# Bounds loaded one behind each gate-and-up loop, gate and up weights in one transfer, first norm beside the gated projections

## The reference

```python
shift, scale, gate = adaln(c[:, None, :], w_ada, b_ada)
h = rms_norm(x, norm_g) * (1 + scale) + shift
hc = rms_norm(xc, norm_g) * (1 + cscale) + cshift
u = h @ w_in
a_val, a_gate = u[..., :A_WIDTH], u[..., A_WIDTH:AB_Q_OFF]
```

```python
hid = jax.nn.silu(xblk @ w_gate[e]) * (xblk @ w_up[e])
return hid @ w_down[e]
```

## Time and profile before

| | |
|---|---|
| median of 3 runs | 4255.51 us (4252.32 to 4255.72) |
| profiled execution | 4245.79 us, its span 4243.7 us |
| mean granted clock of TensorE | 0.965 |
| TensorE busy | 3750.0 us (88%) |
| VectorE, ScalarE, GpSimd busy | 41%, 23%, 6% |
| HBM read and written | 594.70 MB and 46.92 MB |
| gate and up loads by ScalarE | 120, 2048 KB each, 16.6 us from issue to landing |
| down loads by ScalarE | 60, 2048 KB each, 17.2 us |
| write of zeros to y_tok | 12800 KB, 36.3 us |

### The profile page before, as it was taken

The page is one execution under the profiler, slowest core; times in us unless marked ns, Lnnn a source line. Parts: engine busy times, 40 slices in busy tenths (PEclk is TensorE's granted clock), DMA queues, the critical chain, the costliest instruction groups (busy, mean ns, idle before and its releaser), DMA issues.

```text
span 4243.7 us, 81332 instructions
## 1 busy us (share of the span) xinstructions
PE 3750.0 (88%) x29964; PEld 2095.4 (49%) x29965; DVE 1724.6 (41%) x3835; ACT 975.1 (23%) x2286; POOL 272.6 (6%) x453
## 2 busy tenths in 40 slices
PE   5997888999999889999988969989499998899874
PEld 3564665555444555444565445555344444455443
DVE  2585666413202664152465334434331114343335
ACT  3003545302001332131053212222120002222211
POOL 0000000000000000000000021111100000211111
PEclk9998999999999999999999989999799998999997
DMA  8111222101101000110142178999511113799994
GB/s 314 44 40 40 100 88 113 70 24 40 59 20 40 1 1 11 50 48 31 60 160 102 75 283 354 425 426 425 221 40 40 40 61 120 318 366 418 426 426 150
DMA packets 94333, 644.11 MB, mean 152 GB/s; under 512 B 18640, under 2 KB 41240, under 8 KB 60752
## 3 DMA queue, kind: packets, MB, share of 16 engines
q10 hardware_dynamic: 28896, 386.28, 21.5%
q1 hardware_dynamic: 46928, 194.98, 12.4%
q0 software_dynamic: 18336, 60.44, 4.1%
HBM read 594.70 MB, written 46.92 MB: 151 GB/s over the span
## 4 chain that ended last, share of the span: by engine, by line
PE 37%; DMA 13%; DVE 4%; issue 3%; SPq 2%; ACT 1%; DVEq 1%; ACTq 1%; POOLq 0%; POOL 0%
PE banks L258 23%; DMA y_tok<-arena 7%; PE banks L2407 7%; DMA arena<-in_w_gu 4%; SPq L2360 2%; PE banks L2416 2%; DMA arena<-y_tok,arena 1%; PE banks L1519 1%; DVE arena L1634 1%; PE banks L2122 1%; PE banks L2402 1%; PE banks L467 1%; DMA h_tok<-arena 0%; PE banks L2398 0%; ACTq L2300 0%
## 5 line engine op out<-in xcount | busy, mean ns | idle before, releaser
L258 PE MATMUL banks<-arena 128*128 128x512 f32 (+2 forms) x4544 | 1750.0, 547 | 39.0 <-ACTq L137 16.9
L258 PEld LDWEIGHTS banks<-arena 128*128 128x128 f32 x4544 | 841.4, 191 | 935.6 <-issue 884.6
L2407 PE MATMUL banks<-arena 128*32 128x256 f32 x10240 | 611.1, 387 | 48.2 <-DMA arena<-in_w_gu 41.1
L2407 PEld LDWEIGHTS banks<-arena 128*32 128x32 f32 x10240 | 324.4, 111 | 278.9 <-issue 104.8
L2416 PE MATMUL banks<-arena 128*32 128x256 f32 x5120 | 302.5, 384 | 65.4 <-DVE arena L2561 40.9
L2416 PEld LDWEIGHTS banks<-arena 128*32 128x32 f32 x5120 | 167.8, 110 | 194.0 <-DVE arena L2561 94.3
L1588 PE MATMUL banks<-arena 128*64 128x128 f32 x1952 | 161.8, 285 | 54.9 <-ACT arena L1601 39.2
L945 DVE SCALAR_TENSOR_TENSOR arena<-arena 128x1024 f32<-128x1024 f32 x240 | 195.9, 879 | 0.2 <-DVEq L137 0.2
L301 DVE SCALAR_TENSOR_TENSOR arena<-banks,arena 128x512 f32<-128x512 f32 (+1 forms) x72 | 51.9, 721 | 333.3 <-PE banks L258 333.3
L2373 POOL DMA_INDIRECT arena<-h_tok,arena x176 | 172.1, 978 | 142.2 <-POOL arena L2370 141.4
L1519 PE MATMUL banks<-arena 64*128 64x256 f32 (+2 forms) x768 | 130.1, 470 | 37.7 <-ACT arena L1690 32.8
(11 more groups left out here) (327 smaller groups left out, 3500.8 us busy)
## 6 DMA issues: line engine op xcount, KB each, us to landing
arena<-in_w_gu ACTq DMA_DIRECT2D x120, 2048.0 KB, 16.6
arena<-in_w_dn ACTq DMA_DIRECT2D x60, 2048.0 KB, 17.2
arena<-in_w_ada SPq DMA_DIRECT2D x24, 2048.0 KB, 7.3
y_tok<-arena SPq DMA_DIRECT2D x648, 32.0 KB
arena<-in_w_gu SPq DMA_DIRECT2D x8, 2048.0 KB, 10.8
y_tok<-arena POOLq DMA_DIRECT2D x1, 12800.0 KB, 36.3
arena<-in_ab_w_ada SPq DMA_DIRECT2D x6, 2048.0 KB, 9.5
arena<-in_cd_w_ada SPq DMA_DIRECT2D x6, 2048.0 KB, 7.3
```

The source lines that it names most:

```text
L258: last = pe.matmul(self.bank_of(g, n), lhsT, rhs, start=k == 0, stop=k == KT - 1)
L2407: last = pe.matmul(bank(2 + j)[32 * q:32 * q + 32, 0:256], xbT[:, 128 * j + 32 * q2:128 * j + 32 * q2 + 32], w_gu[slot][j][:, 4 * q2 + q], ...
```

## The change

Three edits. **The stage `ab_norm` goes.** TensorE takes the projection with `N_AB` as its norm, so it waits for each tile of h (`nrm_h`) when it first needs it. GpSimd's small memsets come before the close of `ab_mod`, so the scratch of `M_AB` moves by 10240 words, and the zeros wait for VectorE's last division.

**Gate and up are one transfer** of 128 rows of 32768 B, with one semaphore for each slot. **The bounds are read one at a time:** of the two that each engine read behind the gate-and-up loop of the odd expert, the second is now read behind that of the even one.

```diff
-        M_AB = Mods(("ab",), STAGE)
+        M_AB = Mods(("ab",), STAGE + 10240)
...
                     for k in range(KT):
                         a.wait_ge(nrm_x, KT * i + k + 1)
                         a.activation(h_of[w_][:, k, t0:t0 + n], h_of[w_][:, k, t0:t0 + n], ACT.Identity,
-                                     scale=self.scale(k, w_), bias=self.shift(k, w_))
+                                     scale=self.scale(k, w_), bias=self.shift(k, w_)).then_inc(nrm_h, 1)
+
+            def made(self, rows, k):
+                i = 2 if rows[1] is h_c else rows[2] // 512
+                return KT * i + k + 1
...
-            def load_gu(self, eng, slot, e, part):
-                eng.dma_start(mem(SLOTS[slot] + UNIT * part, UNIT),
-                              t["w_gu"][self.l, bass.ds(e, 1), :, UNIT * part:UNIT * part + UNIT].rearrange(
-                                  "e p n -> p (e n)")).then_inc((self.wa, self.wb)[part][slot], 16)
+            def load_gu(self, eng, slot, e):
+                eng.dma_start(mem(SLOTS[slot], 2 * UNIT), t["w_gu"][self.l, bass.ds(e, 1)].rearrange("e p n -> p (e n)")
+                              ).then_inc(self.wg[slot], 16)
...
                     c0, c1, c2 = bring()
-                    c3, c4 = first(2 * p + 1, 1, c1, c2, p, lambda: [self.cum(eng, 2 * p + 3), self.cum(eng, 2 * p + 4)])
+                    c3 = first(2 * p + 1, 1, c1, c2, p, lambda: self.cum(eng, 2 * p + 3))
                     second(2 * p, 0, c0, c1, p)
-                    first(2 * p + 2, 0, c2, c3, p + 1)
+                    c4 = first(2 * p + 2, 0, c2, c3, p + 1, lambda: self.cum(eng, 2 * p + 4))
                     second(2 * p + 1, 1, c1, c2, p)
                     carry((c2, c3, c4))
...
                     nth = i // 2 if nth is None else nth
-                    pe.wait_ge(self.wa[slot], 16 * nth + 16)
-                    pe.sem_inc(passed, 1)
-                    pe.wait_ge(self.wb[slot], 16 * nth + 16)
+                    pe.wait_ge(self.wg[slot], 16 * nth + 16)
                     pe.sem_inc(passed, 1)
...
                     if following:
-                        for part in range(2):
-                            self.load_gu(a, slot, e, part)
+                        self.load_gu(a, slot, e)
...
             mod_pe(pe, N_AB)
             close("ab_mod")
-            close("ab_norm")
-            P_AB_A.pe(pe)
+            P_AB_A.pe(pe, N_AB)
             close("ab_gated")
...
             N_AB.act(a)
-            close("ab_norm")
             P_AB_A.act(a)
...
             N_AB.divide(d, 2)
-            close("ab_norm")
             conv = conv_dve(d)
...
-            close("ab_mod")
             for ct in range(4):
                 for a0, n in ((0, HALF), (HALF + S, 2 * HALF), (S + L + 3 * HALF, HALF)):
                     g.memset(G_U[:, ct, a0:a0 + n], 0.0)
-            close("ab_norm")
-
+            close("ab_mod")
+            g.wait_ge(nrm_x, nrm_total[0])
             g.memset(zeros, 0.0).then_inc(pool_done, 1)
```

More of the change, by code:

```diff
@@ L536, in mod_dve @@
             M_AB.finish(d, link)
-        nrm_sq, nrm_mm, nrm_rt, nrm_x, nrm_rc = (sem(s_) for s_ in ("nrm_sq", "nrm_mm", "nrm_rt", "nrm_x", "nrm_rc"))
+        nrm_sq, nrm_mm, nrm_rt, nrm_x, nrm_rc, nrm_h = (
+            sem(s_) for s_ in ("nrm_sq", "nrm_mm", "nrm_rt", "nrm_x", "nrm_rc", "nrm_h"))
         nrm_total = [0, 0]
@@ L583, in act @@
                         a.activation(h_of[w_][:, k, t0:t0 + n], h_of[w_][:, k, t0:t0 + n], ACT.Identity,
-                                     scale=self.scale(k, w_), bias=self.shift(k, w_))
+                                     scale=self.scale(k, w_), bias=self.shift(k, w_)).then_inc(nrm_h, 1)
+            def made(self, rows, k):
+                i = 2 if rows[1] is h_c else rows[2] // 512
+                return KT * i + k + 1
         N_AB = Norm(True, lambda k, w_: gs["ab"][:, k, w_:w_ + 1], lambda k, w_: mod["ab"][:, k, w_:w_ + 1])
-        nrm_h, nrm_add, nrm_rd = sem("nrm_h"), sem("nrm_add"), sem("nrm_rd")
-        flow = dict(sq=nrm_total[0], mm=nrm_total[1], rt=nrm_total[1], rc=nrm_total[1], x=nrm_total[0], h=0, add=0,
+        nrm_add, nrm_rd = sem("nrm_add"), sem("nrm_rd")
+        flow = dict(sq=nrm_total[0], mm=nrm_total[1], rt=nrm_total[1], rc=nrm_total[1], x=nrm_total[0], h=nrm_total[0], add=0,
                     rd=0)
@@ L2081, in __init__ @@
                 s = block_sem
-                self.wa, self.wb, self.wd = ([s(f"{w_}_slot{j}") for j in range(2)]
-                                             for w_ in ("w_half_a", "w_half_b", "w_down"))
+                self.wg, self.wd = ([s(f"{w_}_slot{j}") for j in range(2)] for w_ in ("w_gate_up", "w_down"))
                 self.ix, self.xg = s("ix"), [sem(f"moe{l}_x_gathered{i}") for i in range(4)]
@@ L2331, in in_turn @@
                 c0, c1, c2 = bring()
-                c3, c4 = first(E - 3, 1, c1, c2, None, lambda: [self.cum(eng, E - 1), self.cum(eng, E)])
+                c3 = first(E - 3, 1, c1, c2, None, lambda: self.cum(eng, E - 1))
                 second(E - 4, 0, c0, c1)
-                first(E - 2, 0, c2, c3)
+                c4 = first(E - 2, 0, c2, c3, None, lambda: self.cum(eng, E))
                 second(E - 3, 1, c1, c2)
@@ L2341, in blocks_sp @@
                 sp.wait_ge(stage_end, closed(("ev_attn", "od_conv")[self.l]))
-                for part in range(2):
-                    self.load_gu(sp, 1, 0, part)
+                self.load_gu(sp, 1, 0)
                 sp.wait_ge(stage_end, closed(("ev_out", "od_out")[self.l]))
-                for part in range(2):
-                    self.load_gu(sp, 0, E - 1, part)
+                self.load_gu(sp, 0, E - 1)
                 self.load_dn(sp, 0, E - 1)
@@ L2952, in _ @@
             close("m1_sum_final")
-STAGES = ["loads", "ab_mod", "ab_norm", "ab_gated", "ab_qkv", "ab_heads", "ab_attn", "ab_z",
+STAGES = ["loads", "ab_mod", "ab_gated", "ab_qkv", "ab_heads", "ab_attn", "ab_z",
           "ab_out_cd_f", "cd_four", "cd_qkv", "cd_attn", "cd_z", "cd_out_ev_in", "ev_attn",
```

## The result

| kernel | median us | of runs | ratio to before, 95% interval |
|---|---|---|---|
| before | 4255.51 | 4252.32 to 4255.72 | |
| changed | 4309.22 | 4305.97 to 4309.56 | 1.0126 [1.0103, 1.0149] |

The account below looks back on a forecast made before the run. In the expert stages full DMA engines, shared packet by packet by weights and stores, nearly balance TensorE; stores end the first. 4245.8 - 12.9 - 5.5 + 41 + 42 = 4310 us, given as 4320 for the median of runs, range 4231 to 4365 us.

Parts of the forecast that it names:

- The sign and the cause: Expert stages: slower, chance 0.65, because a 32 KB weight row is one packet and one turn, leaving stores fewer turns.
- The room: First expert stage: VectorE's room for eight blocks is gone after some four of eleven pairs, then VectorE and TensorE stop.
- The sum: Whole kernel against the profiled execution: 4245.8 - 12.9 - 5.5 + 41 + 42 = 4310 us.
- the norm: Start of the kernel: TensorE's first projection begins at 63.3 us in place of 76.16 us, 12.9 us sooner.
- The stages: Both expert stages: the long row costs 41 us in the first and 42 us in the second; bounds give back 5.5 us.
- The long row: Expert weights: 32 KB rows as one packet each cost +41 us in the first stage, +42 us in the second.
- The turns: Stores beside full weight queues: 608 turns become 405 in the first stage, a block every 10 us instead of 7.0.
- The bounds: Expert loops where TensorE sets the pace: reading bounds one at a time gains 1.1 us a pair, 5.5 us in all.
- ScalarE's single issue: TensorE's second block after the even expert's gate-and-up loop: ScalarE's eviction comes 0.43 us sooner with one issue.
- That the long row costs no turns: First rival, expert stages: the row is cut or turns go by bytes; 4234 us, faster; chance 0.25.
- That the room of eight blocks absorbs most: Second rival, expert stages: stores catch up, 21 us lost against 18 gained, 4258 us; chance 0.10 together with the third.
- The third rival: Norm and bounds gains aren't there either, with the long row free: 4247 us; chance 0.10 together with the second.

Follow-up runs that it names:

- e_split: The changed kernel with gate and up again in two transfers of 2 MB, norm and bounds as changed: 4233.93 us, ratio 0.9962 to before.
- e_one_alone: The kernel before with only the gate and up transfers joined, norm and bounds as before: 4324.09 us, ratio 1.0181 to before.
- e_bounds_alone: The kernel before with only the second bound read behind the even expert's gate-and-up loop: 4242.84 us, ratio 0.9988 to before.
- e_pieces4: The changed kernel with all expert weights in rows of 4 KB: 4248.99 us, ratio 1.0001 to before.
- e_pieces8: The changed kernel with gate-and-up and down weights in rows of 8 KB: 4228.76 us, ratio 0.9953 to before.
- e_pieces16: The changed kernel with the one gate-and-up transfer cut into rows of 16 KB: 4239.95 us, ratio 0.9983 to before.

## Why the prediction was right

**The sign and the cause** were right, and the steps show in the order given: one packet for a row of 32 KB, fewer turns for the stores, VectorE out of room, TensorE behind it, the weights' queue empty. The room was to be gone after four pairs of the full stretch; the first hole, at 2700 us, is in the third.

**The sum** was made against the profiled execution, 4310 us, and the changed kernel's took 4305.97. Of its terms the norm shows at the start of the first expert stage (2460.3 for 2473.1 us, 12.8 for 12.9). That it is so near is luck: the changed kernel's first product began at 64.27 us, 11.9 us sooner, and the other profiles with this edit stood 6 to 14 us ahead at that later place. The stages were given 41 + 42 - 5.5 = 77.5 us and took, stretch and tail together, 35.1 + 2.6 + 25.1 + 11.1 = 73.9 us. Most of the 11 us between 4320 and the median of 4309.22 lies in the 9.7 us added for the median of the kernel before: the changed kernel's median stood only 3.3 us over its profiled execution. That the rest is so near is in part luck, since cost and gains were both put too high: 83 - 18.4 = 64.6 us were forecast between the medians, and 68.0 - 14.3 = 53.7 us came, by the measures of the next two paragraphs.

**The long row**, 83 us, was somewhat too large: 75.8 us by medians when it is the only edit. On top of norm and bounds it is 53.7 + 14.3 = 68.0 us if each kernel is held against its own before, and 75.3 us if the medians of the changed kernel and of `e_split` are subtracted; the three runs of before that stand in the result are what divides the two. The turns came near their size: from 27 to 18 a block should have gone from 7.0 to 10.5 us beside full queues ("every 10 us"), and it took 8.9 to 10.1 us in the full stretches read above. q1 moved 1.21 packets for each of q10 in the first of them (a part of this is the start of the stretch: the kernel before has 1.10 from 2621 to 2690 us and 1.03 over the whole), then 1.06 from 2820 to 2900 us, 1.09 and 1.05 in the later ones. What gives the stores the few extra ones stays open.

**The gains.** The prediction took the norm's 12.9 us whole to the end of the kernel, through a stage that it had itself shown to end with its stores; alone it is worth 6.3 us in the time. The bounds were given 5.5 us and measured 5.8, but that they agree is in part luck: in the one profile all of it lies in the second stage, where 2.2 us were forecast. The wait was to fall to 0.6 us and is at most 0.4 in the rows of `e_bounds_alone`. And ScalarE's single issue was weighed only for one block of the bounds' term (0.43 us sooner). By TensorE's waits it is worth some 5 us a stage beside few stores, an estimate. How much of it was in this result isn't shown: here TensorE waited 13.1 us for ScalarE's evictions in the first stage, up to 5.6 us at a time, and in the hole shown above ScalarE's eviction had itself waited 9.58 us for VectorE's addition.

**The rivals.** That the long row costs no turns is excluded by the packet count and by `e_one_alone`. Its time, 4234 us, is what `e_split`, without the long rows, has (4233.93 us), and that is luck: it was 21.7 us under the kernel before, and `e_split` is 14.3 us under its own, whose median was 7 us lower. That the room of eight blocks absorbs most fell too: the second stage, which the stores had never held, lost as much as the first (36.2 us with its tail, for 37.7). The third rival needed a long row that costs nothing, and fell with the first. The Trainium skill's rule (DMA: Bandwidth & Descriptors, Queues, rings and completion order) that an engine drains a packet of typically 9 to 17 descriptors before it switches would make the row's length of little weight; the 75.8 us of `e_one_alone` and the 8.9 to 10.1 us for 7.0 speak against it for these queues.

## What to carry to other kernels

Where two queues share the transfer engines, count turns and not bytes: joining transfers makes rows longer, and each longer row stands in the way of every short packet of the other queue. Look which queue ends last, and set the row length for that one; here the best was neither the longest nor the shortest. A saving ahead of such a stage can be worth less in the time than at its place: 12.9 us became 6.3 (3.8 to 11.5), though no run shows where the rest went.

## What the runs showed of the hardware

- Rows of 4, 8, 16 and 32 KB each went as one packet: q10's packets were 97056, 50976, 27936 and 20256 (`e_pieces4`, `e_pieces8`, `e_pieces16`, changed), 60 x 16 x (rows and semaphores of an expert on an engine) + 2976 each time.
- Beside a full weight queue the other queue moved 1.03 packets for each of it with 16 KB rows, 1.05 to 1.21 with rows of 32 and 16 KB (the changed kernel's full stretches). Its block of 192 small packets took 7.0 us in the first case and 8.9 to 10.1 us in the second.
- Shorter rows cost little rate: 426 GB/s at 16 KB, 419 at 8 KB, 409 at 4 KB in full slices of the span.
- With the holes in TensorE's work its granted clock fell, 1.00 to 0.95 over the stretch, and the same 5184 products of the gate-and-up loops took 317.1 us in place of 307.1.
